# Four weight slots placed 0, 16, 32 and 48 bytes off a 64-byte grid: a two-layer transformer block on one core

## What is computed

```python
h = h + 0.5 * swiglu(rmsnorm(h, ffn1_norm[i]), ffn1_w_gate[i], ffn1_w_up[i], ffn1_w_down[i])
...
h = h + jnp.concatenate([attn_o, gla_o], axis=-1) @ w_out[i]
h = h + 0.5 * swiglu(rmsnorm(h, ffn2_norm[i]), ffn2_w_gate[i], ffn2_w_up[i], ffn2_w_down[i])
gate = jax.nn.sigmoid(rmsnorm(h, ple_gate_norm[i]) @ ple_w_gate[i])
emb = rmsnorm(p[i] @ ple_w_proj[i], ple_norm[i])
...
x = x + even_mixer(...)            # or odd_mixer
x = x + mem_attention(...)         # 4 heads over 256 memory tokens
x = x + conv_ffn(...)              # x @ w_up (5632 wide), conv, gate, @ w_down
```

## The kernel before

| tile | start modulo 64 | start modulo 512 |
|---|---|---|
| `op_hi`, `op_lo` | 0 | 128 |
| `w_hi`, `w_lo`, each slot and each 128x128 tile in it | 0 | 128 |
| `h_hi`, `h_lo`, `mix_hi`, `query_hi`, `x`, `w_raw` | 0 | 128 |
| `sums_r` (matrices of ones), `sums_hi`, `tmp` | 0 | 384 |
| `sq`, `sums_lo`, `rs` | 32 | 352 |
| `pl_hi`, `pl_lo`, `cr_mhi`, `cr_mlo`, `even_hi`, `sil`, `conv_buf` | 32 | 416 |

## Time and profile before

### The profile page before, as it was taken

The page is one execution under the profiler, slowest core; times in us unless marked ns, Lnnn a source line. Parts: engine busy times, 40 slices in busy tenths (PEclk is TensorE's granted clock), DMA queues, the critical chain, the costliest instruction groups (busy, mean ns, idle before and its releaser), DMA issues.

```text
span 2561.3 us, 31974 instructions
## 1 busy us (share of the span) xinstructions
PE 2541.6 (99%) x12548; PEld 2107.0 (82%) x12548; DVE 1596.4 (62%) x1976; ACT 912.6 (36%) x1184; POOL 10.2 (0%) x24
## 2 busy tenths in 40 slices
PE   8999999999999999999999999999999999999999
PEld 7888888778888888877898888888886888888887
DVE  6444468866444468677765747476357665775755
ACT  5222234543222245344443423233146343432322
POOL 0000001000000000000000000000000000000000
PEclk9999999999999999999999999999999999999999
DMA  5222233112222232212321232323210232232222
GB/s 182 102 83 99 96 110 120 67 50 96 103 89 98 99 115 101 99 50 99 132 94 63 104 103 82 115 83 123 94 66 13 87 116 83 84 115 83 101 96 82
DMA packets 37410, 241.91 MB, mean 94 GB/s; under 512 B 4416, under 2 KB 7280, under 8 KB 9136
## 3 DMA queue, kind: packets, MB, share of 16 engines
q1 hardware_dynamic: 34736, 233.78, 26.3%
q10 hardware_dynamic: 1920, 5.22, 0.6%
q0 software_dynamic: 640, 1.31, 0.2%
HBM read 236.89 MB, written 2.10 MB: 93 GB/s over the span
## 4 chain that ended last, share of the span: by engine, by line
PE 93%; DVE 5%; ACT 1%; issue 1%; DMA 0%; POOL 0%; DVEq 0%; ACTq 0%
PE ps L605 24%; PE ps L607 24%; PE ps L606 24%; PE ps L1234 1%; PE ps L623 1%; PE ps L625 1%; PE ps L624 1%; PE ps L766 1%; PE ps L1267 1%; PE ps L1291 1%; PE ps L1282 1%; DVE w_lo L2048 1%; PE ps L768 1%; PE ps L767 1%; PE ps L1303 1%
## 5 line engine op out<-in xcount | busy, mean ns | idle before, releaser
L605 PE MATMUL ps<-op_hi,w_hi 128*128 128x512 f32 x2056 | 800.9, 390 | 0.2 <-DVE op_lo L1929 0.2
L606 PE MATMUL ps<-op_lo,w_hi 128*128 128x512 f32 x2056 | 800.5, 389 | 0.0
L607 PE MATMUL ps<-op_hi,w_lo 128*128 128x512 f32 x2056 | 800.4, 389 | 0.0
L1350 ACT ACTIVATE w_hi<-w_raw 128x2048 fp32r<-128x2048 f32 x217 | 414.4, 1911 | 485.2 <-PE ps L607 315.3
L2048 DVE TENSOR_TENSOR w_lo<-w_raw,w_hi 128x2048 fp32r<-128x2048 f32 x217 | 497.0, 2292 | 38.7 <-ACT w_hi L1350 22.3
L605 PEld LDWEIGHTS ps<-op_hi,w_hi 128*128 128x128 f32 x2056 | 386.3, 188 | 81.4 <-issue 1.4
L607 PEld LDWEIGHTS ps<-op_hi,w_lo 128*128 128x128 f32 x2056 | 386.2, 188 | 80.6
L606 PEld LDWEIGHTS ps<-op_lo,w_hi 128*128 128x128 f32 x2056 | 386.3, 188 | 80.3
L2013 DVE SCALAR_TENSOR_TENSOR x<-ps,x 128x512 f32<-128x512 f32 x134 | 92.7, 691 | 310.8 <-PE ps L607 293.0
L605 PE MATMUL ps<-h_hi,w_hi 128*128 128x512 f32 x692 | 269.5, 389 | 0.0
L606 PE MATMUL ps<-h_lo,w_hi 128*128 128x512 f32 x692 | 269.2, 389 | 0.0
(11 more groups left out here) (373 smaller groups left out, 3085.7 us busy)
## 6 DMA issues: line engine op xcount, KB each, us to landing
w_raw<-in_wstream_dram SPq DMA_DIRECT2D x217, 1024.0 KB, 4.8
cr_m<-in_mem_dram ACTq DMA_DIRECT2D x2, 1024.0 KB, 4.9
w_raw<-in_wstream_dram SPq DMA_DIRECT2D x7, 256.0 KB, 8.0
x<-in_x_dram SPq DMA_DIRECT2D x3, 512.0 KB, 7.3
out_dram<-x SPq DMA_DIRECT2D x3, 512.0 KB, 2.6
m_s<-m_q POOLq DMA_DIRECT2D x16, 64.0 KB, 2.5
ev_s<-in_alibi_dram ACTq DMA_DIRECT2D x1, 1024.0 KB, 4.9
m_c<-in_rope_dram ACTq DMA_DIRECT2D x1, 640.0 KB, 3.9
```

Source lines behind the costliest of these rows:

```text
L605: mm_(o, w_hi[:, c % 4, w], hi[:, k, 0:cols], start=(k == 0), stop=False)
L606: mm_(o, w_hi[:, c % 4, w], lo[:, k, 0:cols], start=False, stop=False)
L607: mm = mm_(o, w_lo[:, c % 4, w], hi[:, k, 0:cols], start=False, stop=(k == kt - 1))
L1350: f_(w_hi[:, c % 4, :], w_raw[:, c % 2, :], ACT.Copy).then_inc(w_hi_ready, 1)
```

## The change

It alters where tiles lie and nothing else. A slot of `w_hi` and `w_lo` gets 4 more float32 at its end (16 bytes) that nobody uses, so slot 0, 1, 2 and 3 begin 0, 16, 32 and 48 bytes further modulo 64. A filler of 448 bytes ahead of `w_lo` brings `w_lo` to the same place modulo 512 as `w_hi`. `op_hi` and `op_lo` lie ahead of the weights and stay. All that is declared behind `w_lo` moves by 576 bytes, which is 64 modulo 512 and 0 modulo 64: `h_hi`, `h_lo`, `x`, `w_raw`, `pl_hi`, `cr_mhi` and the rest. Instructions, their order, their shapes and their waits are the same on every engine; only line numbers behind the edit rise by one.

```diff
         op_hi = sb("op_hi", [P, KT, SEQ], FP32R)
         op_lo = sb("op_lo", [P, KT, SEQ], FP32R)
-        w_hi = sb("w_hi", [P, 4, SLAB], FP32R)
-        w_lo = sb("w_lo", [P, 4, SLAB], FP32R)
+        w_hi = sb("w_hi", [P, 4, SLAB + 4], FP32R)[:, :, 0:SLAB]
+        sb("before_w_lo", [P, 112])
+        w_lo = sb("w_lo", [P, 4, SLAB + 4], FP32R)[:, :, 0:SLAB]
```

## The result

The changed kernel takes 2593.5 us (2593.29 to 2593.75, 2 runs) against 2562.1 us: a ratio of 1.0122, 95% interval 1.0093 to 1.0152. The prediction was 2590.7 us, within 2%. The span of the profiled execution is 2591.5 us, 30.2 us more than before.

A forecast was written before the change was run, and what follows sets the result against it. TensorE was taken as the bound. Terms 13.8 (slot 2) + 13.6 (slots 1 and 3) + 1.5 (other 512-column matmuls) - 0.3 (embeddings) gave +28.6 us, so 2590.7 us, range 2540 to 2622 us.

The forecast's parts named there:

- What bounds the kernel: TensorE, busy 99% of the span, is the bound; only the rate at which matmuls follow each other can move.
- A distance between the operands costs, and 32 bytes cost 6.7 ns: L605 to L607 in slot 2: 233.3 against 226.7 ns per 512-column matmul, 2,061 of them, +13.8 us.
- Slots 1 and 3 at 230 ns: L605 to L607 in slots 1 and 3: 230.0 ns, +3.3 ns for each of 4,122 matmuls, +13.6 us.
- Inner values 64 bytes further cost 0: h_hi and h_lo 64 bytes further modulo 512: 0 us; if 64 did matter, 3.5 us either way.
- the embeddings: 48 matmuls with slab 78 in slot 2 come to distance 0 and 226.7 ns: -6.7 ns each, -0.3 us.
- Others with 512 columns: L766 and its like, 768 matmuls: three quarters may lose the regular state, up to 1.9 us, taken as +1.5 us.
- 256 columns 0: Some 1,500 matmuls with 256 moving columns: some gain, some lose, 5.6 us at most either way, taken as 0.
- The 0.8 us from span to time: The median of the runs stands 0.8 us above the span, so a span of 2589.9 becomes 2590.7 us.
- Rival 1: Any distance but 0 loses the regular state; L605 to L607 in slots 1 and 3 at 235.7 ns: 2615 us, chance 0.17.
- Rival 2: Placement within 64 bytes has no steady effect; L708 and even_hi are slow for another reason: 2562 us, chance 0.12.
- rival 3: A shift separates two colliding reads, saving up to 13.3 ns per matmul: 2480, 2521 or mildly 2554 us; chance 0.15.
- The Trainium skill's sentence: Streaming operand and weight load have independent read ports, so placement would change nothing and the time stays.

The follow-up runs named there:

- Experiment 3: Everything from op_hi on moved 32 bytes further than in the kernel before, all distances between operands kept: 2562.3 us, ratio 1.0000.
- Experiment 1: Kernel before with weights unmoved and only what lies behind w_lo, h_hi and h_lo included, 64 bytes further modulo 512: 2569.0 us, ratio 1.0027.
- experiment 2: All four slots of w_hi and w_lo 16 bytes further than in the kernel before, the rest in place modulo 512: 2613.4 us, ratio 1.0199.
- Experiments 6: Kernel before, placement kept; in to_features the middle matmul of three loads only 64 of 128 weight columns: 2587.5 us, ratio 1.0098.
- experiment 9: Kernel before, placement kept; in to_features the six middle k of eight (four of six) load 64 of 128 weight columns: 2582.8 us, ratio 1.0081.
- experiment 12: All four weight slots 144 bytes further than in the kernel before (distance +112): 2581.6, 2591.9, 2603.0 and 2593.0 us in four runs, ratio 1.0132.

## Why the prediction was right, point by point

- **What bounds the kernel.** TensorE's rate, nothing else: +30.2 us of span against +31.6 us of busy PE, and L2049 and L1351 unchanged. Right.
- **A distance between the operands costs, and 32 bytes cost 6.7 ns.** Right: slot 2 has 233.1 ns, with op (-32) and with h (+32). Experiment 3 shows that it is the distance, which before the change two groups at one place had only suggested.
- **Slots 1 and 3 at 230 ns.** Right as a mean, by luck, and wrong in each part. The value was the middle between two neighbours, with no row at either distance. Over all MLP slabs slot 1 has a mean of 229.2 ns and slot 3 of 231.5, together 230.3. In the MLP tabled above, slot 3 with op has 233.5, slot 1 has 226.7 or 233.3, and with h they have 231.9 and 228.8. "One of the two finds the regular state again and the other wanders" is close to what happens in the up slabs. The 27.4 us of slots 1 to 3 were 30.1 for the three lines, of which h is 7.8 and op 22.2; part of that is slot 0 with h, which had been put at 0.
- **Inner values 64 bytes further cost 0, "everything else that I saw went with the distance modulo 64".** This step failed. Experiment 1 gives it 6.9 us by itself, above the 3.5 us that had been set as its bound: the bound counted slot 0 of the changed kernel only, and by itself the shift meets all four slots. For the same reason the embeddings gained 4 ns (233.3 to 228.9) and not 6.7. The evidence for modulo 64 was one pair, 0 and 256; the pair fits 256 as well, and I had no row at 64 or 128. In the changed kernel itself the wrong step costs little: slot 0 of h, 519 x 2.3 ns = 1.2 us.
- **Others with 512 columns +1.5 us, 256 columns 0.** Measured +1.3 and -1.9. (The others are 804 with the 48 of the embeddings, so 756 and not 768, which changes nothing.)
- **The 0.8 us from span to time.** In every run whose time and span are both on record the time is about 1.8 us above the span, so the 0.8 joined two executions. It is 1 us of the 2.8 by which the forecast fell short.
- **Rival 1** (no distance but 0 can keep the regular state, 2615 us): wrong for this kernel, but experiment 2, with 2613.4 us, has nearly its time, by another sum: 233.3 ns in all four slots and not 235.7 in two. What it missed is that the state is inherited. **Rival 2** (placement does nothing) and **rival 3** (the shift takes the reads apart): refuted; of some twenty distances none was below 226.7.
- **The Trainium skill's sentence** that loading weights does not steal read bandwidth from the running matmul ("TensorE: Matmul & The Clock Gate", Part 2) would have given no change. The runs do not agree with what follows from it for placement: moving the weights alone costs up to 2% (experiment 2), and moving both costs nothing (experiment 3).

**What stays open.** Why it is 226.7 ns. The theory tested after the result was interference of the weight load, growing with its length. Experiments 6 and 9 do not bear this out, since half the columns did not lessen the time. No run had a matmul with no load beside it, so a fixed price for the exchange of weights is not told apart from interference that does not grow with the load. Nor is it shown what it is that a stretch inherits, or why in the runs seen +4 finds the regular state behind a slow slab, +112 finds it in some MLPs and not in another, and -16 never finds it by itself. A rule that gives the pitch from the distance and from what came before was not found: +16 has 227.1 and 228.8 ns in one run, each time behind a slab at +32. The period of 256 bytes fits all pairs measured within 0.3 ns but one, 128 and -128, which differ by 0.9.

## What to carry to other kernels

Where TensorE is the bound and every matmul has its own weight load, as here, try first to give the moving and the stationary tiles the same place modulo 256 bytes, and check the pitch (first start, last start, count), not the duration. A pad that looks harmless cost 0.3 to 2% here by this alone (experiments 1 and 2). Only fp32r matmuls with 512 columns were measured for this. Do not judge a placement by one stretch: at some distances the pitch is 226.7 or 233.3 ns for hundreds of us by how the stretch began, and the time of one and the same program can differ by 20 us from run to run.

## Not expected of the hardware

- A 512-column matmul with its load runs in a regular state of 226.7 ns (in the kernel before found within 10 matmuls of every break from 28 us on), or else in patterns that repeat, with means of 228.8 to 234.2 ns.
- The state outlives a change of slab, of slot and of moving tile: 340 us in experiment 12.
- Shifts of 4 bytes matter (232.5 ns at -4, 226.8 at +4).
- A smaller weight load (134 instead of 188 ns) in a third of the matmuls of L605 to L607 made the kernel slower by 25 us; in experiment 9 it cost 3.3 ns each, and full loads right behind ran at 226.7 ns again.
